# Spreading the gathered rows over V and forming V's low gate parts two pieces at a time in a one-core decoder layer

## The reference

```python
def peer_ffn(xn, w_pq, sub_keys, expert_u, expert_v):
    q = (xt @ w_pq).reshape(T, PEER_HEADS, 2, PEER_HALF_DIM)
    s = jnp.einsum('thpd,hpkd->thpk', q, sub_keys)
    ...                                    # top 16 of 16*16 sums: 8 heads * 16 experts per token
    gates = jax.nn.softmax(top_s, axis=-1)
    u = jnp.take(expert_u, eb, axis=0)
    act = jax.nn.gelu(jnp.einsum('tkd,td->tk', u, xb), approximate=False)
    v = jnp.take(expert_v, eb, axis=0)
    return jnp.einsum('tk,tkd->td', gb * act, v)
```

## Time and profile before

| what | value |
|---|---|
| median of three runs | 1897.89 us |
| profiled execution | 1897.14 us, span 1895.3 us |
| TensorE, matmuls busy | 1871.6 us, 99% |
| VectorE busy | 1391.9 us, 73% |
| ScalarE busy | 944.6 us, 50% |
| GpSimd busy | 1229.4 us, 65% |
| matmuls of stage V | from 1237.1 us to 1881.7 us |
| DMA in stage V | 327 to 391 GB/s in the 40 us stretches up to 1800 us, against some 200 in stage U from 600 us on |

### The profile page before, as it was taken

One profiled execution on the slowest core, in us unless ns is written; L12 is line 12 of the kernel. 1 busy time (PEld: TensorE's weight loads), 2 busy tenths in 40 slices (PEclk: granted clock), 3 DMA queues, 4 the chain that ended last, 5 costly groups with the idle time before them and its releaser, 6 DMA issues.

```text
span 1895.3 us, 33337 instructions
## 1 busy us (share of the span) xinstructions
PE 1871.6 (99%) x11798; PEld 1759.4 (93%) x11798; DVE 1391.9 (73%) x2303; ACT 944.6 (50%) x1342; POOL 1229.4 (65%) x538
## 2 busy tenths in 40 slices
PE   9999999999999999999999999999999999999997
PEld 7888889888999999999999999989999999999997
DVE  8534685045635777948888888279999989999987
ACT  7453355474544444544444444445555555555555
POOL 3867768877898999999999999952222213243401
PEclk9999999999999999999999999999999999999999
DMA  9544646654754565555555555689999988999984
GB/s 332 187 144 148 202 142 227 193 189 155 218 180 178 214 220 207 211 200 200 196 195 196 199 198 198 216 300 372 388 384 385 377 352 345 378 380 371 372 310 142
DMA packets 83299, 473.99 MB, mean 250 GB/s; under 512 B 9630, under 2 KB 12574, under 8 KB 38302
## 3 DMA queue, kind: packets, MB, share of 16 engines
q1 hardware_dynamic: 65288, 367.30, 54.4%
q0 software_dynamic: 12384, 90.18, 12.2%
q10 hardware_dynamic: 5552, 15.51, 2.6%
HBM read 468.07 MB, written 4.19 MB: 249 GB/s over the span
## 4 chain that ended last, share of the span: by engine, by line
PE 49%; POOL 29%; issue 11%; DVE 5%; DMA 5%; ACT 1%; POOLq 0%; SPq 0%; DVEq 0%; ACTq 0%
POOL wlo L466 28%; PE ps L1915 15%; PE ps L2016 14%; PE ps L1918 8%; PE ps L2019 8%; DMA raw<-in_w_v 4%; DVE wlo L1468 2%; PE ps L1929 1%; DVE big L1483 1%; ACT whi L566 1%; PE ps L1615 1%; PE ps L1617 1%; PE ps L1616 1%; POOL wlo L500 1%; DVE gate_parts L1470 1%
## 5 line engine op out<-in xcount | busy, mean ns | idle before, releaser
L566 ACT ACTIVATE whi<-raw 128x1024 fp32r<-128x1024 f32 x691 | 732.5, 1060 | 918.7 <-PE ps L1918 348.7
L466 POOL TENSOR_TENSOR wlo<-raw,whi 128x1024 fp32r<-128x1024 f32 x428 | 1037.2, 2431 | 193.1 <-ACT whi L566 187.0
L1915 PE MATMUL ps<-x_parts,whi 128*128 128x428 f32 x2048 | 577.5, 363 | 1.8 <-POOL wlo L466 1.8
L2016 PE MATMUL ps<-gate_parts,whi 128*128 128x428 f32 x2000 | 567.4, 364 | 5.8 <-DVE gate_parts L1470 3.1
L1918 PEld LDWEIGHTS ps<-x_parts,wlo 128*128 128x128 f32 x2048 | 384.1, 188 | 15.7
L2019 PEld LDWEIGHTS ps<-gate_parts,wlo 128*128 128x128 f32 x2000 | 375.6, 188 | 15.1
L1918 PE MATMUL ps<-x_parts,wlo 128*128 128x214 f32 x2048 | 382.5, 268 | 0.0
L2019 PE MATMUL ps<-gate_parts,wlo 128*128 128x214 f32 x2000 | 373.9, 268 | 0.0
L1468 DVE TENSOR_TENSOR wlo<-raw,whi 128x1024 fp32r<-128x1024 f32 x248 | 302.4, 1220 | 39.8 <-ACT whi L566 39.4
L1915 PEld LDWEIGHTS ps<-x_parts,whi 128*128 128x128 f32 x2048 | 310.5, 191 | 2.2 <-POOL wlo L466 2.2
L2016 PEld LDWEIGHTS ps<-gate_parts,whi 128*128 128x128 f32 x2000 | 303.2, 192 | 9.5 <-issue 3.8
(11 more groups left out here) (260 smaller groups left out, 2092.9 us busy)
## 6 DMA issues: line engine op xcount, KB each, us to landing
raw<-in_w_u SPq DMA_DIRECT2D x128, 1024.0 KB, 4.8
raw<-in_w_v SPq DMA_DIRECT2D x128, 1024.0 KB, 8.7
raw<-in_w_front SPq DMA_DIRECT2D x180, 512.0 KB, 3.6
big<-in_mem ACTq DMA_DIRECT2D x8, 256.0 KB, 6.1
big<-in_mem_t ACTq DMA_DIRECT2D x2, 1024.0 KB, 6.0
big<-in_x ACTq DMA_DIRECT2D x2, 1024.0 KB, 8.2
x_back<-x2t_scratch ACTq DMA_DIRECT2D x2, 856.0 KB, 9.4
big<-in_x_t SPq DMA_DIRECT2D x3, 512.0 KB, 7.7
```

The source lines that it names most:

```text
L466: nc.gpsimd.tensor_tensor(wlo[:, j % SPL, :], raw[:, j % RAW, :], whi[:, j % SPL, :], ALU.subtract).then_inc(lo_done, 1)
L566: nc.scalar.activation(whi[:, (base + j) % SPL, :], raw[:, (base + j) % RAW, :], ACT.Copy).then_inc(hi_done, 1)
L1915: nc.tensor.matmul(sums[:, 0:2 * TD], whi[:, s, cols], x_parts[:, :, m, 0:TD], start=m == 0, stop=False, skip_group_check=True)
L2016: nc.tensor.matmul(sums[:, 0:2 * TD], whi[:, s, cols], gate_parts[:, g, :, 0:TD], start=False, stop=False, skip_group_check=True)
```

## The change

Four things are changed.

1. `taken` is spread wider: rows of U are taken after pieces 9 to 122 in place of 15 to 118, rows of V after pieces 128 to 238 in place of 128 to 232. The gain row is loaded at piece 3, straight behind the x of the sparse tokens, and they are multiplied after piece 8 in place of 13.
2. VectorE forms the low gate parts of pieces j and j + 1 with one instruction of 2 x 214 columns, for even j. `gate_parts` has four places (GPL) in place of three, and the two halves of a place, 214 columns each, now lie against each other, where before 42 unused columns lay between them. ScalarE's `gated_high` runs one piece ahead.
3. The addends of the sparse tokens are loaded at piece 241 in place of 236, behind the residual's transfer at piece 240, and `add_group` comes after pieces 244, 246 and 251 in place of 240, 241 and 251.
4. Some scratch columns of `stats` move, to make room.

The core of the diff:

```diff
-SPL = 3
+SPL, GPL = 3, 4
...
-ROWS_FROM, WEIGHTS_AT_PIECE, ROWS_UNTIL = 15, 127, 234
-ADDED_AT = (*range(240, 239 + GROUPS), 251)
+GAINED_AT, ROWS_FROM, WEIGHTS_AT_PIECE, ROWS_UNTIL = 8, 9, 127, 240
+ADDED_AT = (*range(244, 242 + 2 * GROUPS, 2), 251)
...
-        return ROWS_FROM + n * (WEIGHTS_AT_PIECE - 6 - ROWS_FROM) // PER
+        return ROWS_FROM + n * (WEIGHTS_AT_PIECE - 2 - ROWS_FROM) // PER
...
-        gate_parts = sb("gate_parts", [P, SPL, 2, T], F32R)
+        gate_parts = sb("gate_parts", [P, GPL, 2, TD], F32R)
...
             for j in range(BODY):
                 high_v(LAST_BODY, j)
-                gated_high(LAST_BODY * BODY - NK, j)
+                gated_high(LAST_BODY * BODY - NK, j + 1)
                 if j == 0:
                     load_back(1)
-                if j == 3:
+                if j == 1:
+                    act.wait_ge(rows_taken, 2 * PER)
+                    load_addend(0)
+                    load_addend(1)
+                if j == 6:
                     for k in range(2, GROUPS):
                         act.wait_ge(group_added, k - 1)
                         load_addend(k)
...
-                dve.wait_ge(ghi_done, j + 1)
-                nc.vector.tensor_tensor(gate_parts[:, j % SPL, 1, 0:TD], W[:, j % NK, :], gate_parts[:, j % SPL, 0, 0:TD],
-                                        ALU.subtract).then_inc(glo_done, 1)
+                if j % 2 == 0:
+                    dve.wait_ge(ghi_done, j + 2)
+                    two = slice(j % GPL, j % GPL + 2)
+                    nc.vector.tensor_tensor(gate_parts[:, two, 1, :], W[:, j % NK:j % NK + 2, :], gate_parts[:, two, 0, :],
+                                            ALU.subtract).then_inc(glo_done, 1)
...
-                if j == 13:
+                if j == GAINED_AT:
...
-                pe.wait_ge(glo_done, i * BODY + (j + 1))
+                pe.wait_ge(glo_done, i * (BODY // 2) + (j // 2 + 1))
```

More of the change, by code:

```diff
@@ L810, in _ @@
                     high_v(i, j)
-                    gated_high(i * BODY - NK, j)
+                    gated_high(i * BODY - NK, j + 1)
             for j in range(BODY):
                 high_v(LAST_BODY - 1, j)
-                gated_high((LAST_BODY - 1) * BODY - NK, j)
-                if j == 8:
+                gated_high((LAST_BODY - 1) * BODY - NK, j + 1)
+            for j in range(BODY):
+                high_v(LAST_BODY, j)
+                gated_high(LAST_BODY * BODY - NK, j + 1)
+                if j == 0:
+                    load_back(1)
+                if j == 1:
                     act.wait_ge(rows_taken, 2 * PER)
@@ L818, in _ @@
                     load_addend(1)
-            for j in range(BODY):
-                high_v(LAST_BODY, j)
-                gated_high(LAST_BODY * BODY - NK, j)
-                if j == 0:
-                    load_back(1)
-                if j == 3:
+                if j == 6:
                     for k in range(2, GROUPS):
@@ L2055, in _ @@
                         pe.wait_ge(first_joined, c + 1)
-                    ins = v_block((V0 + j) % SPL, c, first=j > last_first, last=j == last_first)
+                    ins = v_block(FOLD_BODY * BODY + j, c, first=j > last_first, last=j == last_first)
                     if j == last_first and c < 7:
```

55 lines of the change are left out of this document (28 added, 27 removed).

## The result

The changed kernel takes 1910.52 us (median of 4 runs, 1907.46 to 1913.23) where the kernel before, beside it, takes 1896.11 (4 runs): ratio 1.0068, 95% interval 1.0048 to 1.0087. It is slower, beyond the interval, 17.7 us above the prediction and outside its range (1888 to 1899). The profiled execution took 1908.91 us.

The account below looks back on a forecast made before the run. TensorE was taken to bound the kernel, with V at the edge of the DMA and near VectorE's. Terms -1.6 - 3.5 + 0.2 + 0.5 + 0 - 0.3 = -4.7 us gave 1892.8 us, range 1888 to 1899.

Parts of the forecast that it names:

- the change touches stage V alone: Whole kernel: only what stops TensorE can be won or lost, and only in stage V; no term for the front.
- C: Rival, V's matmuls: joined gate halves make the 428 columns quicker, up to 28 us over 2048 blocks, 1869 us; chance 0.05.
- The relief: Stage V: spreading the rows lowers DMA demand by 4% in the first half and 3% in the second.
- 46.7 us: ScalarE's idle time for weight loads between 1580 and 1830 us; it was to fall well below this.
- Steady part, first half: V's first half behind the opening: two thirds of 2.4 us lost would go, -1.6 us.
- Second half and end: V after 1563.61 us: two thirds of 5.3 us lost would go, -3.5 us.
- rival A: V: weight loads are late by bunching, so stops stay; only opening, addends and tail count, +0.4 us, 1897.5 us; chance 0.23.
- Opening: V's first pieces: GpSimd's three waits stay, VectorE's stops shift slightly; +0.2 us, bounds -0.8 and +3.
- rival B: V's opening: VectorE's product waits for the gain row, holding weights and gathers; about +7.5 us, 1904.6 us; chance 0.10.
- Gates in pairs: V, VectorE: one gate instruction for two pieces, 0.51 us in place of 0.58, saves 9 us of VectorE's time beside TensorE's work.
- Fold, addends, tail: Piece 128's sums 0; addends behind the residual's transfer +0.5 us; end of the kernel 0.3 us earlier.
- step of V: V's undisturbed pace, 0.6133 us for two blocks; a change in it would show the prediction wrong.

Follow-up runs that it names:

- f1: The changed kernel with `stats` cut to 208 columns, so `x_parts` lies at distance 0 from `whi`: 1898.97 us (10 runs), ratio 0.9999 to the kernel before.
- e2: The kernel before with `stats` of 248 columns in place of 240, moving every tile behind it by 32 bytes: 1907.25 us (5 runs), ratio 1.006.
- e7: The kernel before with more padding behind the gates, so that `x_parts` alone moves by 256 bytes: 1896.31 us (one execution).
- g3: The kernel before with a 32-byte gap ahead of `whi`, so `whi`, `wlo` and `x_parts` all move together: 1895.71 us (one execution).
- g1: The changed kernel, unaltered, run once more: 1907.57 us (6 runs), ratio 1.0052 to the kernel before.
- e1: The changed kernel with `stats` 32 bytes shorter (224 columns), so tiles behind it start on multiples of 64 bytes: 1903.89 us (10 runs), ratio 1.0038 to before.
- e3: The kernel before with the change's rows, gain row and addends, but single gates and all tiles in place: 1897.58 us (10 runs), ratio 1.0014.
- g2: f1 with the gates alone 32 bytes lower (`stats` of 200 columns, a gap of 8 behind `gate_parts`): 1899.37 us (10 runs), ratio 1.0015 to before.
- f3: The kernel before with `x_parts` alone 64 bytes further on, a repeat of e5: 1896.92 us, ratio 0.9999.
- e4: e1 with the rows, gain row and addends of before, leaving the gate pairs alone: 1901.97 us (10 runs), ratio 1.0028 to the kernel before.
- f2: f1 with the rows, gain row and addends of before, leaving the gate pairs alone: 1898.61 us, ratio 1.0008 to the kernel before.
- f4: The kernel before with only the one-hot tables and gate parts moved by 32 bytes, a repeat of e8: 1898.51 us, ratio 1.0005.
- e8: The kernel before with `stats` of 248 columns and 32 bytes less padding, so gates move by 32 bytes and `x_parts` stays: 1900.04 us (one execution).
- g4: The kernel before with a 32-byte gap ahead of `wlo`, so all but `whi` move: 1903.3 us (one execution).
- e5: The kernel before with 64 bytes more padding behind the gates, so `x_parts` alone moves: 1898.52 us (one execution).

## Why the prediction was wrong

**The step that failed is one that the sum did not have.** I counted instructions, waits and transfers, and costed the layout at nothing: "the change touches stage V alone". The change's own list said that scratch columns of `stats` move to make room, and `gate_parts` grew by 448 bytes, padding included. What it costs in the front is 8.0 us by the landmarks (7.4 us + 1.4 us = 8.8 us by the paces). The runs bear it out. f1 has distance 0, not 192: between it and the change the front's own difference is 466.5 - 457.2 = 9.3 us, and the whole kernels, each against its own before, differ by (1907.57 - 1896.01) - (1898.97 - 1896.73) = 9.3 us. With the address mended, the change makes no difference that the runs can show (0.9999). That the distance of the operands matters is shown (e2, e7, g3, f1); why it does is not: no view shows what TensorE's reads wait for.

**A second failure stands behind it.** Even f1 took 1898.97 us, 6 us above the forecast: V gave nothing of the -4.7. V from its first piece to its end took 644.6 us in the profile before, 645.7 in the changed kernel; over all executions profiled with the rows of before 644.7 on average, over the six with the change's rows (the change, g1, e1, e3, f1, g2) 645.9. Time lost against 2.453 us a piece, for all kernels alike:

```
                                  before  after   f1    g1
pieces 1 to 13 (opening)             4.6    6.7   6.8   8.1
pieces 14 to 126                     2.4    2.9   3.7  -0.2
pieces 127, 128                      3.1    2.7   2.7   2.7
pieces 129 to 252                    6.3   5.35   5.5   5.8
full pace of one piece, us         2.453  2.441 2.447 2.441
```

A loss below nothing shows that 2.453 is not the full pace of every kernel, hence the last row; more on it under *C*.

- *The relief came in the first half alone.* In the 260 us from 43 us after V's first matmul (1280 to 1540 in the earlier trace rows, 1291 to 1551 after) the DMA moved 371 GB/s in place of 384, a weight pair took 8.5 us to land in place of 8.9, and ScalarE waited 29.2 us for weights in place of 48.0. Before and after:

```profile
L566 ACT ACTIVATE whi<-raw 128x1024 fp32r<-128x1024 f32 x105 | 111.4, 1061 | 121.2 <-PE ps L2019 72.9 <-DMA raw<-in_w_v 48.0
```

```profile
L565 ACT ACTIVATE whi<-raw 128x1024 fp32r<-128x1024 f32 x105 | 111.3, 1060 | 121.0 <-PE ps L2023 91.8 <-DMA raw<-in_w_v 29.2
```

```profile
DMA packets 13274, 96.55 MB, mean 371 GB/s; under 512 B 1470, under 2 KB 1470, under 8 KB 1598
...
raw<-in_w_v SPq DMA_DIRECT2D x52, 1024.0 KB, 8.5
```

  Over all profiles that wait is 41 to 61 us with the rows of before (14 executions) and 8 to 43 with the change's (6). In the second half the prediction read 46.7 us, and after it is 20.9:

```profile
L565 ACT ACTIVATE whi<-raw 128x1024 fp32r<-128x1024 f32 x101 | 107.1, 1061 | 117.7 <-PE ps L2023 96.7 <-DMA raw<-in_w_v 20.9
```

  But this is no gain of the change: the same window of the other 13 executions with the rows of before shows 12.7 to 43.5 us (12.7 in f3, the row below), 25.8 on average with before's own, and the six with the change's rows 26.7. The 46.7 was the largest of all.

```profile
L566 ACT ACTIVATE whi<-raw 128x1024 fp32r<-128x1024 f32 x101 | 107.2, 1062 | 115.8 <-PE ps L2019 103.0 <-DMA raw<-in_w_v 12.7
```

- *Steady part, first half (-1.6 forecast).* Before's own execution was a lucky one: all 14 with the rows of before lose between 2.4 and 6.4 us in pieces 14 to 126, 4.7 on average; the six with the change's rows -0.2 to 3.7, 2.1 on average. The gain is some 2.5 us, 1 of it pace, so the relief is worth about what was forecast, but it can be seen only against many executions. The opening takes it back.
- *Second half and end (-3.5).* Not to be had. Of before's 6.3 us, 1.0 lies in piece 129, where its granted clock was down; the 5.3 that are left stand beside 5.3 in the changed kernel. Over all executions pieces 130 to 252 lose 3.8 us on average with the rows of before (2.4 to 6.5) and 5.5 with the change's (3.8 to 8.4). So rival A's number for V was nearly right. TensorE's waits from 1250 us on (as the earlier trace rows; a step's wait is now mostly put down to the weight part, L1471):

```profile
PE ps L2020 <- DVE wlo L1471: 6.3, 9, 1.3
PE ps L2020 <- POOL wlo L499: 3.0, 3, 1.1
PE ps L2020 <- DVE gate_parts L1475: 1.6, 3, 1.1
```

- *Opening (+0.2).* This term was mis-sized: 6.7 us are lost in after and 8.1 in g1, so +2.1 and +3.5 us, against 4.6 (4.4 to 5.0 in all executions with the rows of before and single gates). The gate pairs alone (e4, f2) lose 5.1 to 5.2 us before piece 14, e3 with the rows alone 8.1. So early rows and gain row cost some 3 us, the pairs 0.5. The first is the DMA. TensorE, ScalarE and VectorE of the changed kernel:

```profile
1267.00 0.62 PE L2020 MATMUL ps<-gate_parts,whi 128*128 128x428 f32 x2 [1.00 <-POOL wlo L499]
...
1275.49 0.62 PE L2020 MATMUL ps<-gate_parts,whi 128*128 128x428 f32 x2 [0.85 <-DVE wlo L1471]
...
1279.26 0.65 PE L2020 MATMUL ps<-gate_parts,whi 128*128 128x428 f32 x2 [1.08 <-DVE gate_parts L1475]
```

```profile
1269.05 1.06 ACT L565 ACTIVATE whi<-raw 128x1024 fp32r<-128x1024 f32 x1 [5.23 <-DMA raw<-in_w_v]
```

```profile
1251.10 2.35 DVE L1475 TENSOR_TENSOR gate_parts<-big,gate_parts 128x428 fp32r<-128x428 f32 x1 [1.14 <-ACT gate_parts L761]
...
1260.10 3.53 DVE L1475 TENSOR_TENSOR gate_parts<-big,gate_parts 128x428 fp32r<-128x428 f32 x1 [3.92 <-ACT gate_parts L761]
...
1270.14 1.23 DVE L1471 TENSOR_TENSOR wlo<-raw,whi 128x1024 fp32r<-128x1024 f32 x1 [6.51 <-ACT whi L565]
1271.29 0.60 DVE L1475 TENSOR_TENSOR gate_parts<-big,gate_parts 128x428 fp32r<-128x428 f32 x1
1271.80 2.28 DVE L1550 TENSOR_TENSOR big<-x_back,big 126x2048 f32<-126x2048 f32 x1
```

  ScalarE waits 5.23 us for the weights of piece 8, and VectorE, idle for 6.51 us, is late from its first weight part on. In all six executions with the change's rows this wait is 5.2 to 7.2 us (7.18 in e3), in before and f2 2.5 and 2.3. Up to that piece the gain row is the only transfer that the edit moved, so it is the one in the way. I had counted VectorE's work and whether the gain row would be in time; what it did to the weight pair behind it I priced only in rival B. The gain row took 15.2 us to land, not the 12.3 of the earlier trace rows. And the pairs are held while GpSimd works as the single ones were: 2.35 and 3.53 us in place of 0.60.

- *Gates in pairs.* Right in size: 0.60 us for 428 columns (the forecast, 0.29 + 0.22, was for the time to the next instruction's start, and 1271.80 - 1271.29 is 0.51), and VectorE's busy time fell. No run shows a saving from it on TensorE's path.
- *Fold, addends, tail.* Pieces 127 and 128 lose 2.7 us in place of 3.1. That is the clock, not the change: in eight executions, before's among them, the granted clock is 0.50 for some 3 us there (first row below; after, second row, it stays at 1.00), and these lose 3.0 to 3.2 us and another 0.6 to 1.2 in piece 129. The other twelve lose 2.7 and nothing. Both kinds of kernel are in both groups.

```profile
1562.50:1565.50 3.00, 3.00 (x10) 2.85 (x11) 3.00 (x4) 1.33 (x2) 0.00 (x0) 0.50 0.77 289
```

```profile
1570.00:1580.00 10.00, 8.91 (x50) 7.10 (x48) 10.00 (x14) 3.93 (x7) 0.94 (x1) 1.00 0.73 272
```

  From piece 253 to the end of the span it is 20.5 us in place of 21.2 (1907.1 - 1886.56 and 1895.3 - 1874.11), 0.6 sooner, but in the other five executions with the change's rows 20.8 to 21.2: the 0.3 forecast isn't there to be seen. The residual landed in 4.5 us, not 8.1, so the addends behind it were in no one's way.

**The rivals.** *A* is what V did: its +0.4 us stands nearest to the +1.1 measured for V, and f1's ratio of 0.9999 is its 1897.5. *B* had the sign and nearly the form: the gain row's megabyte does collide with the weights. But its mechanism is not there: the product, at 1271.80, shows no wait for the gain row, the cost is 2.1 to 3.5 us and not 7.5, and the rest of its sign is the front's.

*C* has the direction right and the size wrong. The changed kernel runs 44 pieces of V (13 to 56) without a stop in 107.40 us, 2.441 us a piece or 0.610 for two blocks, where the earlier trace rows has 0.6133; f4 has the gates one by one but 32 bytes off, and 28 pieces (46 to 73) take it 69.00 us, 2.464 a piece:

```profile
1286.86 0.57 PE L2020 MATMUL ps<-gate_parts,whi 128*128 128x428 f32 x2
...
1394.26 0.56 PE L2020 MATMUL ps<-gate_parts,whi 128*128 128x428 f32 x2
```

```profile
1356.21 0.57 PE L2016 MATMUL ps<-gate_parts,whi 128*128 128x428 f32 x2
...
1425.21 0.56 PE L2016 MATMUL ps<-gate_parts,whi 128*128 128x428 f32 x2
```

So the step of V did change, which the prediction had named as a sign that it would be wrong, and the gates' place explains part of it. With single gates and 192 bytes from `whi` to the gates all nine kernels have 2.453, g3 too, where everything moved by 32 bytes together; at 224 bytes e2, e8 and f4 have 2.464; g4, with `whi` at 224 and `wlo` at 192, has 2.459. With pairs the four places lie at four different distances, and the pace of a piece repeats every four pieces: 2.449, 2.461, 2.437, 2.439 in f1 and the same in f2; 2.425, 2.454, 2.457, 2.450 in e1 and e4; 2.448, 2.439, 2.429, 2.444 in the change and g1. How much of the gain in pairs comes from the joined halves and how much from the distances, no run separates. Over 256 pieces the change gains 256 x (2.453 - 2.441) = 3 us by it (C had up to 28), and V is no shorter: so its stops cost that much more.

**Open.** Why the stops of V grow as its pace does (VectorE has less room between two pieces then, but no run tests it); whether the change has a part in the slow start; the distance of 160 bytes. The gates' own address, 32 bytes off a multiple of 64, costs 256 x 0.011 = 2.7 us where gates are single, which fits V's 647.5 and 648.0 us in e8 and f4 against 644.7; e2 has the same pace, but few stops and 644.0. In g2 the pace is 2.450 and it is stops that make V 648.8. No kernel run here beats the kernel before: f1 and f3 tie with it.

## What to carry to other kernels

When a change alters a tile's size, write down which tiles move and by how many bytes, also those of stages that the diff doesn't touch; and when a time surprises, compare the start of every stage and the pace of an undisturbed stretch in each before looking into the stage that was edited. To try an edit fairly, pad so that the distances between operands stay as they were, or run the kernel before with the new layout alone. Relief on an upstream queue is worth only what reaches the bounding engine, and one execution's stops and waits are too few to size it: here 2.4 us in one profile were 4.7 on average, and a wait of 46.7 us was 25.8. And measure the full pace of each kernel before you lay one ruler on all.

## What the runs showed of the hardware

- With fp32r operands, TensorE's pace for matmuls of 512 columns depended on the distance between stationary and moving operand in SBUF modulo 256 bytes: 0.682 us for three at 0, 0.687 at 192, 0.698 to 0.703 at 32, 64, 96, 128 and 224, up to 3%. Stage U as a whole (matmuls of 428 and 214 columns, x_parts moving) didn't follow: 666.6 us before, 666.9 after, 663.6 to 667.3 in all, in no order of the distance.
- V's pace (428 and 214 columns, gates moving, weights stationary) did: 2.453 us a piece at 192 bytes, 2.464 at 224, and with four gate places at four distances a pattern that repeats every four pieces (2.425 to 2.461).
- At the start of the front none to some 14 matmuls of 512 columns stood 0.43 us apart in place of 0.23, up to some 3 us, and their number differed between executions of one kernel (none in e5, eight in f3). Where the view shows the clock of such a stretch (f1), it is 0.50.
- Between its halves V lost another 1.4 us or so where the granted clock was 0.50 for some 3 us after TensorE's stops for the banks' sums: 8 of 20 executions.
